# Attention heads in pairs through a three-step loop, with bias, scale and maximum fused, in a float32 transformer kernel

## What is computed

```python
def global_gqa(q, k, v):                 # 8 heads, 2 key heads, all 256 keys
    s = einsum(q, k) * d ** -0.5
    p = softmax(s, axis=-1)
    return einsum(p, v)

def window_gqa_sink(q, k, v, sink):      # 8 heads, only keys within 128 tokens
    s = where(valid, einsum(q, k) * d ** -0.5, -inf)
    m = maximum(s.max(-1, keepdims=True), sink)
    p = exp(s - m)
    p = p / (p.sum(-1, keepdims=True) + exp(sink - m))
    return einsum(p, v)

def mixer_ab(h, ...):                    # layer 0: both kinds of head, side by side
    return concatenate([global_gqa(...), window_gqa_sink(...)]) @ w_out

def mixer_c(h, w_in, w_out, rpb):        # layer 1: 16 heads, neighbourhood of the
    s = einsum(q, k) * d ** -0.5 + bias  # 64-wide grid, bias by relative position
    return einsum(softmax(s), v) @ w_out

def memory_attn(h, mem, ...):            # both layers: 4 heads of width 256
    return einsum(softmax(einsum(q, k) * 256 ** -0.5), v) @ w_o

for i in range(2):                       # the second block
    x = layer_norm(alpha * x + 0.5 * swiglu(x))
    x = layer_norm(alpha * x + (mixer_ab(x) if i == 0 else mixer_c(x)))
    x = layer_norm(alpha * x + memory_attn(x, mem))
    x = layer_norm(alpha * x + 0.5 * swiglu(x))
```

## Time and profile before

| | |
|---|---|
| three executions, median | 2832.29 us (2828.89 to 2833.37) |
| the profiled execution, its own time | 2827.79 us |
| its span in the trace | 2826.3 us |
| TensorE busy | 2672.8 us, 95% |
| VectorE, ScalarE, GpSimd busy | 66%, 51%, 6% |
| granted TensorE clock, mean | 0.979 of full |

### The profile page before, as it was taken

The page is one execution under the profiler, slowest core; times in us unless marked ns, Lnnn a source line. Parts: engine busy times, 40 slices in busy tenths (PEclk is TensorE's granted clock), DMA queues, the critical chain, the costliest instruction groups (busy, mean ns, idle before and its releaser), DMA issues.

```text
span 2826.3 us, 30383 instructions
## 1 busy us (share of the span) xinstructions
PE 2672.8 (95%) x12593; PEld 2169.4 (77%) x12593; DVE 1867.2 (66%) x1877; ACT 1437.8 (51%) x1495; POOL 159.9 (6%) x161
## 2 busy tenths in 40 slices
PE   7999996999999999999998998899999999899998
PEld 5788774878787777778786886597887887678886
DVE  4655565888887887888787557556555544754644
ACT  4444344767676676767674444434443343534432
POOL 2200120000000000000000002000000004200000
PEclk9999997999999999999999999899999999999999
DMA  6555443999998999999996544054655547244652
GB/s 234 182 188 187 159 165 132 364 312 365 318 365 306 349 332 313 359 314 364 309 364 225 198 160 164 16 209 164 200 187 170 203 135 207 92 149 149 208 183 70
DMA packets 451171, 640.75 MB, mean 227 GB/s; under 512 B 16084, under 2 KB 358144, under 8 KB 451024
## 3 DMA queue, kind: packets, MB, share of 16 engines
q1 hardware_dynamic: 444528, 618.52, 64.3%
q0 software_dynamic: 6496, 20.20, 2.5%
HBM read 637.61 MB, written 1.05 MB: 226 GB/s over the span
## 4 chain that ended last, share of the span: by engine, by line
PE 82%; DVE 11%; ACT 4%; DMA 2%; issue 1%; POOL 0%; SPq 0%; DVEq 0%
PE bank L475 25%; PE bank L477 25%; PE bank L476 25%; DVE part_lo L464 5%; ACT part_hi L456 2%; PE bank L964 1%; PE bank L782 1%; DMA raw<-in_c_w_in_dram 1%; PE bank L635 1%; PE bank L1006 1%; PE bank L487 1%; PE bank L808 1%; DMA raw<-in_w_in_dram 1%; DVE x_rows L1967 1%; POOL rstd L2022 0%
## 5 line engine op out<-in xcount | busy, mean ns | idle before, releaser
L464 DVE TENSOR_TENSOR part_lo<-raw,part_hi 128x2048 fp32r<-128x2048 f32 x587 | 1335.7, 2294 | 397.1 <-ACT part_hi L456 396.8
L456 ACT ACTIVATE part_hi<-raw 128x2048 fp32r<-128x2048 f32 x587 | 1107.5, 1911 | 46.4 <-DMA raw<-in_c_w_in_dram 18.4
L475 PE MATMUL bank<-part_hi,x_hi 128*128 128x512 f32 x1088 | 446.1, 410 | 17.8 <-DVE part_lo L464 14.1
L477 PE MATMUL bank<-part_hi,x_lo 128*128 128x512 f32 x1088 | 435.6, 400 | 0.0
L476 PE MATMUL bank<-part_lo,x_hi 128*128 128x512 f32 x1088 | 433.8, 399 | 0.0
L475 PE MATMUL bank<-part_hi,hT_hi 128*128 128x512 f32 x888 | 351.8, 396 | 19.2 <-DVE hT_lo L1438 19.0
L475 PE MATMUL bank<-part_hi,expert_in_hi 128*128 128x512 f32 x896 | 364.4, 407 | 1.6 <-DVE expert_in_lo L1438 1.6
L476 PE MATMUL bank<-part_lo,expert_in_hi 128*128 128x512 f32 x896 | 355.9, 397 | 0.0
L477 PE MATMUL bank<-part_hi,expert_in_lo 128*128 128x512 f32 x896 | 355.5, 397 | 0.0
L476 PE MATMUL bank<-part_lo,hT_hi 128*128 128x512 f32 x888 | 350.4, 395 | 0.0
L477 PE MATMUL bank<-part_hi,hT_lo 128*128 128x512 f32 x888 | 348.2, 392 | 0.0
(11 more groups left out here) (263 smaller groups left out, 2730.2 us busy)
## 6 DMA issues: line engine op xcount, KB each, us to landing
raw<-in_exp_w_gate_dram SPq DMA_DIRECT2D x224, 512.0 KB, 4.9
raw<-in_exp_w_up_dram SPq DMA_DIRECT2D x224, 512.0 KB, 6.6
raw<-in_exp_w_down_dram SPq DMA_DIRECT2D x112, 1024.0 KB, 7.0
raw<-in_ffn_w_gate_dram SPq DMA_DIRECT2D x110, 512.0 KB, 3.8
raw<-in_ffn_w_up_dram SPq DMA_DIRECT2D x110, 512.0 KB, 5.1
raw<-in_ffn_w_down_dram SPq DMA_DIRECT2D x55, 1024.0 KB, 4.9
raw<-in_w_in_dram SPq DMA_DIRECT2D x20, 1024.0 KB, 5.2
raw<-in_mem_w_kv_dram SPq DMA_DIRECT2D x16, 1024.0 KB, 5.1
```

The source lines that it names most:

```text
L456: p.nc.scalar.activation(p.part_hi[i][:, :], p.raw[i][:, :], ACT.Copy).then_inc(*self.rounded.step((name,)))
L464: p.nc.vector.tensor_tensor(p.part_lo[i][:, :], p.raw[i][:, :], p.part_hi[i][:, :].bitcast(F32), ALU.subtract).then_inc(*self.split.step(( ...
L475: nc.tensor.matmul(out, stat_hi, move_hi, start=start, stop=False, skip_group_check=True)
L477: return nc.tensor.matmul(out, stat_lo, move_hi, start=False, stop=stop, skip_group_check=True)
```

## The change

The heads of `ab` and `c` go through the loop in pairs (`PAIRS`), those of `mem` singly (`SINGLES`). An item, a pair or a single head, goes through three steps in place of four, and a fourth buffer `p3` is added. Scores are made one item ahead. In a pair the two heads' score matmuls alternate, and so do the two heads' products with v. On VectorE one `tensor_tensor_reduce` for each 256 columns takes the place of scale and bias, maximum and negation: it makes -scale * (scores + bias) and its running minimum, which is minus the maximum. So the bias and the masks carry a factor 8 (for `c` GpSimd multiplies each head's bias first, one more operation for each of the 16 heads), heads without a bias add a constant zero, the sink comes in as the minimum's start, and `Exp` reads `p` for all heads, where it read the bank for heads without a bias. The other work in the loops is placed anew, by item; in `c` the first three parts of the q projection stand behind the second pair's scores, where they stood behind the first head's. The out projection takes its four weight blocks by the half of `cat` that they multiply, and then by the half of the output columns. It stays behind the loop: `pe_out_early` and the argument `early` are new and no stage uses them.

```diff
 NFF = D_FF // FC
 AHEAD = 4
...
-        self.ring.square_blocks(st, [(w, c, kh) for w, c in blocks + [(wo, 0), (wo, 512)] for kh in range(2)])
+        self.ring.square_blocks(st, [(w, c, kh) for w, c in blocks for kh in range(2)]
+                                + [(wo, c, kh) for kh in range(2) for c in (0, 512)])
...
+def pe_scores(p, st, heads, item):
...
-    hd, b = heads[i], 4 + i % 2
-    for key in hd["ready"]:
-        pe.wait_ge(*p.s.at(*key))
-    if i >= 2 and heads[i - 2]["bias"] is None:
-        pe.wait_ge(*p.s.at("soft", st, i - 2))
-    elif i >= 2:
-        pe.wait_ge(*p.v.at("biased", st, i - 2))
+    for i in item:
+        for key in heads[i]["ready"]:
+            pe.wait_ge(*p.s.at(*key))
+        if i >= 2:
+            pe.wait_ge(*p.v.at("biased", st, i - 2))
     for qt in range(TT):
-        for j, (q, k) in enumerate(hd["terms"]):
-            mm = nc.tensor.matmul(p.bank[b][:, qt * T:(qt + 1) * T], q[:, qt * P:(qt + 1) * P], k,
-                                  start=(j == 0), stop=(j == len(hd["terms"]) - 1), skip_group_check=True)
-    mm.then_inc(*p.t.step(("scores", st, i)))
...
+    for i in item:
+        pe.wait_ge(*p.s.at("pT", st, i))
...
+    for j in range(heads[item[0]]["out"][2]):
         for kt in range(TT):
-            mm = nc.tensor.matmul(p.bank[b][rows, j * T:(j + 1) * T], hd["v"](kt, j), pT[i % 2][:, kt, :],
-                                  start=(kt == 0), stop=(kt == TT - 1), skip_group_check=True)
-    mm.then_inc(*p.t.step(("weighed", st, i)))
...
+            for i in item:
+                b, rows, parts = heads[i]["out"]
+                mm = nc.tensor.matmul(p.bank[b][rows, j * T:(j + 1) * T], heads[i]["v"](kt, j), pT[i % 2][:, kt, :],
+                                      start=(kt == 0), stop=(kt == TT - 1), skip_group_check=True)
...
+def pe_attention(p, st, heads, items, prob, pT, meanwhile):
+
+    m = len(items)
+    pe_scores(p, st, heads, items[0])
+    for j in range(m + 2):
+        if j + 1 < m:
+            pe_scores(p, st, heads, items[j + 1])
+        if j >= 2:
+            pe_weigh(p, st, heads, pT, items[j - 2], items[j - 4][-1] if j >= 4 else None)
+        if 1 <= j <= m:
+            pe_turn_p(p, st, prob, items[j - 1])
+        for part in meanwhile.get(j, ()):
             part()
-        if 2 <= i <= n + 1:
-            pe_turn_p(p, st, i - 2, prob)
-        if i >= 4 and heads[i - 4]["flush"]:
-            flushed[heads[i - 4]["out"][0]] = i - 4
-        if 3 <= i < n + 3:
-            pe_weigh(p, st, i - 3, heads[i - 3], pT, flushed.get(heads[i - 3]["out"][0]))
-    p.pe.wait_ge(*p.v.at("cat_parts", st, n - 1))
...
     q0, q1 = (pe_transposed_half(p, st, 8, b, 2, "qT") for b in range(2))
     k0, k1 = (pe_transposed_half(p, st, 10, b, 3, "kT") for b in range(2))
     meanwhile = {
-        0: [lambda: first(0), *q0[0:2]], 1: q0[2:3], 2: q0[3:4],
-        3: [lambda: first(1), k0[0]], 4: k0[1:2], 5: k0[2:4],
-        6: [lambda: second("qT", 0), *q1[0:2]], 7: q1[2:4],
-        8: [lambda: second("kT", 0), *k1[0:2]], 9: k1[2:3], 10: k1[3:4],
+        0: [lambda: free("kT", 0, 0), *q0[0:3]], 1: [q0[3], lambda: free("kT", 0, 1), *k0[0:2]], 2: k0[2:4],
+        3: [lambda: free("qT", 1, 0), *q1], 4: [lambda: free("kT", 1, 0), *k1],
     }
...
             for qt in range(TT):
-                src = p.bank[b][:, qt * T:(qt + 1) * T] if hd["bias"] is None else P_[:, qt, :]
-                made = nc.scalar.activation(P_[:, qt, :], src, ACT.Exp, bias=p.att_stats[:, i, 0, qt:qt + 1],
-                                            scale=scale if hd["bias"] is None else 1.0,
-                                            accum_out=p.att_stats[:, i, 1, qt:qt + 1])
+                made = nc.scalar.activation(P_[:, qt, :], P_[:, qt, :], ACT.Exp, bias=p.att_stats[:, i, 0, qt:qt + 1],
+                                            scale=-1.0, accum_out=p.att_stats[:, i, 1, qt:qt + 1])
...
+    m = len(items)
+    for j in range(m + 3):
+        for i in items[j] if j < m else ():
+            hd = heads[i]
             dve.wait_ge(*p.t.at("scores", st, i))
-            if hd["bias"] is None:
-                nc.vector.tensor_reduce(top, p.bank[b][:, :].rearrange("p (q k) -> p q k", q=TT), AX.X, ALU.max).then_inc(
-                    *p.v.step(("max", st, i)))
-                dve.wait_ge(*p.v.at("max", st, i))
-                nc.vector.tensor_scalar(top, top, -scale, None, ALU.mult).then_inc(*p.v.step(("top", st, i)))
-            else:
-                if hd["bias_ready"] is not None:
-                    dve.wait_ge(*p.g.at(*hd["bias_ready"]))
-                if i >= 3:
-                    dve.wait_ge(*p.t.at("p_turned", st, i - 3))
-                for qt in range(TT):
-                    bias = hd["bias"](qt)
-                    rows = lambda ap: ap.rearrange("p (m w) -> p m w", w=bias.shape[2])
-                    made = nc.vector.scalar_tensor_tensor(
-                        out=rows(P_[:, qt, :]), in0=rows(p.bank[b][:, qt * T:(qt + 1) * T]), scalar=scale,
-                        in1=bias, op0=ALU.mult, op1=ALU.add)
-                made.then_inc(*p.v.step(("biased", st, i)))
-                dve.wait_ge(*p.v.at("biased", st, i))
-                nc.vector.tensor_reduce(top, P_[:, :, :], AX.X, ALU.max).then_inc(*p.v.step(("max", st, i)))
-                dve.wait_ge(*p.v.at("max", st, i))
-                if hd["sink"] is None:
-                    nc.vector.tensor_scalar(top, top, -1.0, None, ALU.mult).then_inc(*p.v.step(("top", st, i)))
-                else:
-                    nc.vector.tensor_scalar(top, top, hd["sink"], -1.0, ALU.max, ALU.mult).then_inc(*p.v.step(("top", st, i)))
...
+            if hd["bias_ready"] is not None:
+                dve.wait_ge(*p.g.at(*hd["bias_ready"]))
+            if i >= 4:
+                dve.wait_ge(*p.t.at("p_turned", st, i - 4))
             for qt in range(TT):
...
+                bias = hd["bias"](qt)
+                rows = lambda ap: ap.rearrange("p (m w) -> p m w", w=bias.shape[2])
+                made = nc.vector.tensor_tensor_reduce(
+                    out=rows(prob[i % 4][:, qt, :]), in0=rows(p.bank[4 + i % 2][:, qt * T:(qt + 1) * T]), in1=bias,
+                    scale=-scale, scalar=3e38 if hd["sink"] is None else hd["minus_sink"], op0=ALU.add, op1=ALU.min,
+                    accum_out=p.att_stats[:, i, 0, qt:qt + 1])
+            made.then_inc(*p.v.step(("biased", st, i)))
...
     for h in range(C_HEADS):
-        nc.gpsimd.tensor_tensor(bias[:, h, :, :], bias[:, h, :, :],
-                                p.const("neighbours").unsqueeze(1).to_broadcast([P, BIAS_ROWS, GRID_W]), ALU.add).then_inc(
+        view = bias[:, h, :, :]
+        nc.gpsimd.tensor_scalar(view, view, HD ** 0.5, None, ALU.mult).then_inc(*p.g.step(("wide_bias", st, h)))
+        pool.wait_ge(*p.g.at("wide_bias", st, h))
+        nc.gpsimd.tensor_tensor(
+            view, view, p.const("neighbours").unsqueeze(1).to_broadcast([P, BIAS_ROWS, GRID_W]), ALU.add).then_inc(
             *p.g.step(("bias", st, h)))
```

244 lines of the change are left out of this document (124 added, 120 removed).

## The result

The changed kernel took 2783.51 us (median of four, 2781.57 to 2786.30), the kernel before 2832.83 (four, 2828.89 to 2834.76). The ratio is 0.9828, 95% interval 0.9811 to 0.9845: 49 us faster, where 20 were forecast and 2800 to 2828 was the range. Its profiled execution took 2785.18 us, with a span of 2784.0, 42.3 less than the span of before.

The account below looks back on a forecast made before the run. No engine was seen to fill the loops: heads' steps wait for each other and TensorE's clock falls at times. Terms -9 (`ab`), -11 (`c`) and 0 (the rest) took the median 2832.3 to 2812 us, range 2800 to 2828.

Parts of the forecast that it names:

- The rest: 0.: Outside the `ab` and `c` loops: `mem` 0, between -1 and +2 us each; reordered out projection 0; masks' factor nothing.
- The loop of `ab`: Attention loop of `ab`: later start, then shorter pair steps ending at 1814.3 instead of 1825.9, 11.6 us less, forecast -9.
- the 2.6 us kept back for one more stretch at the low clock: Loop of `ab`: allowance taken off the 11.6 us gain for low clock beyond what the steps hold, leaving -9.
- the lower bound of 0.39: VectorE's fused operation: at least 0.39 us each, from the scale-and-bias operation, accumulator row hidden; 0.50 was taken.
- Bound by VectorE.: Pair step of the loop: about 4.2 us, bound by VectorE with ScalarE and TensorE close behind; `ab` took 8.6 a pair.
- The loop of `c`: Attention loop of `c`: TensorE idle 8.7 us at the start, steps 14 us shorter in all, 3 kept back, forecast -11.
- (1): Rival: VectorE's fused operation runs at the scan's rate, 0.76 us each; gain only -7.5, 2825 us; chance 0.10.
- (2): Rival: pairing gains no overlap, TensorE stays at 5.3 to 5.7 us a pair; about -6, 2826 us; chance 0.08.
- (3): Rival: clock stays at 1.2 GHz through the fast steps, each 6.3 us, not 4.2; +5, 2837 us; chance 0.08.
- (5): Rival: GpSimd's 16 additional operations stop VectorE for their whole 26 us, taking `c`'s gain away; 2823 us; chance 0.05.
- neither stopped dead there: Argument against GpSimd stopping VectorE in `c`: long subtraction and adds stand in the same microseconds, yet neither stopped.
- (4): Rival: more gain, fused operation 0.44 us, no additional low clock, weighing at 1.1; -30, 2802 us; chance 0.12.

Follow-up runs that it names:

- before_shift: The kernel before with 64 bytes of unused memory in front of the ring of weight buffers; ratio 0.9961 to the kernel before.
- after_noshift: The changed kernel with its two small new buffers put behind all others, so the weight ring lies where it lay before; ratio 0.9892 to the kernel before.
- the unfused kernel: The changed kernel with the fused operation undone (scale and bias, maximum and negation again), pairs and steps kept; ratio 0.9910 to the kernel before.
- after_no_multiply: The changed kernel without GpSimd's 16 multiplications of the bias in `c`; ratio 0.9843 to the kernel before.
- after_64: The changed kernel with 96 more bytes ahead of the weight ring, its buffers at 64 from a multiple of 128; ratio 0.9786 to the kernel before.
- after_aligned: The changed kernel with 32 more bytes in front of the weight ring, its buffers at multiples of 128 bytes; ratio 0.9746 to the kernel before.

## Why the prediction was wrong, by its steps

**"The rest: 0."** This step took the result out of the range: without the shift the change is at 0.9892, which is 2802 us and inside it. Nothing outside the loops was priced but the order of the out projection and `mem`. `mem` was near (+0.3 each); the out projections lost 1.6 and 1.8 us to the low clock, which the 0 had not allowed for. Two buffers of 64 bytes together (the change's lines `self.minus_sink = put("minus_sink", [P, 8])` and `self.zero = put("zero", [P, 1])`, which I had left out even of the diff shown ahead of the prediction) move the 9 blocks of the weight ring and all behind them, and that alone is worth 11 us (before_shift) to 18 (after_noshift); the traces support the lower end. No row of before shows it; that it was taken for nothing without a bound was the mistake.

**The loop of `ab`: -9 forecast, -19.8 measured.** This is the largest single miss, 10.8 us, and the trace divides it. The starting point was right: rotations of 6.0 us, TensorE idle behind them, low clock. But the first step ended 15.1 us into the loop and not 18.1: four fused operations took 1.4 us, not 2.0, for each of the two pairs that stand ahead of it, and the step itself was shorter. The next three steps, forecast at 6.0, 4.8 and 4.0, took 4.5, 4.7 and 5.6, the same in sum, by luck. The last five took 18.8 us, not 24.0. The forecast had put a whole subtraction or rounding of 2.2 on top of two of them, but none took over 4.8: the first subtraction fell into the step before and cost it 0.9, the second fell into time in which VectorE would have waited. And the 2.6 us kept back for one more stretch at the low clock did not come. Mis-sized as terms were the fused operation (0.50 taken; 0.35 without and 0.41 with a sink measured, the first kind under the lower bound of 0.39) and the pair's products (1.3 taken, 1.08 measured).

**"Bound by VectorE."** A step of 4.2 us was forecast and 4.5 to 4.7 measured, near enough, but for another reason: TensorE and VectorE take turns in a ring of waits over the four buffers of p, and VectorE is idle 0.9 to 2.0 us in each step that has no subtraction. And what fusion does in `ab` was missed altogether. Its price was put at 1.63 - 1.00 a head of VectorE's time; the unfused kernel loses 17 us in `ab`, 7 of them in heads that save next to nothing on VectorE; there the trace shows the scores waiting for `Exp` to free their bank.

**The loop of `c`: -11 forecast, -14.9 measured** (the steps' own sum was 14). Its mechanism held: second scores waiting for VectorE, here 6.2 us and not 8.7, as the loop starts 28 us earlier and lies otherwise against the subtraction; the two multiplications at 0.9 to 1.7 us beside GpSimd (1.98 assumed); bias in time. That the sum of the steps came so near is partly luck: the first step was 2.2 us shorter than forecast, the next four 1.0 shorter, and the last five, in part at the low clock, 2.4 longer.

**The rivals.** (1), the fused operation at the scan's rate: no, 0.35 to 0.41 each. The Trainium skill's rule on two float32 inputs in SBUF ("Vector Engine (DVE) Microarchitecture Reference", "Points that are easy to get wrong"), by whose letter this rival would not occur with one input in PSUM, is not contradicted; no fused operation here had both inputs in SBUF. (2), no overlap: no, 1.14 and 1.08 at full clock, even without alternation. (3), the low clock through the fast steps: it lasted over some steps of each loop (0.89 and 0.84 granted), and did not decide. (5), GpSimd stopping VectorE for all its length: no, after_no_multiply is no faster, and VectorE's multiplications lose 5.9 us and not 26. But "neither stopped dead there" was a misreading. The 25.9 us of 16 merged additions in the earlier trace rows hide two kinds, about 1.0 us alone and over 3 us when one begins during a subtraction:

```profile
L2124 POOL TENSOR_TENSOR bias<-bias,consts x16: 987/1026/3133, 2396.1 to 2421.0; 128x384 f32<-128x384 f32 x16
```

(4), more gain, came nearest: 34 us in the loops, 30.6 with the out projections' loss, against 30. The rest of the distance was the ring's 64 bytes.

## What to carry to other kernels

When a change adds or resizes a buffer, compare the start times of the same instructions in stretches that it doesn't touch, before crediting the change with the whole difference; and try the placement for itself, since here 32 bytes of padding gave 23 us, where two rewritten loops gave 34. Price a fused operation not only by its engine's time but by which buffer or bank it frees, and how much earlier. Where a step is a ring of waits, taking one wait away shows the next at once: look at the loop's length, not at the wait. And before a mean from a merged row enters an estimate, look whether it mixes two kinds: the 1.6 us of an addition above was 1.0 or 3.0.

## What the runs showed of the hardware

- Matmuls of 512 columns with `x` start 234.2, 233.0, 229.6 and 228.1 ns apart with the weight ring at 32, 96, 64 and 0 bytes from a multiple of 128 (before, before_shift, after_64, after_aligned; no difference in work). In the kernel before, 96 is worth 11 us and 0 is worth 39 us against 32. With `hT` 32 bytes off and the ring at 0 the matmuls with `hT` start 233.0 ns apart, in place of 227.2. Which access is slowed, TensorE's reads or others beside them, was not tried.
- Two heads' matmuls on different halves of the rows or columns run at once when they stand behind one another with no wait between, whether they alternate or not: 1.14 and 1.08 us for eight records (1.14 and 1.09 one head after the other), as for four.
- A VectorE operation with a minimum as accumulator over 256 columns, one input from PSUM and one from SBUF, starts every 0.35 us without and 0.41 with a start value from memory, and its accumulator's write is hidden. The row of 0.48 spans more than the interval, so lengths of rows must not be added.
- VectorE's subtraction (two inputs from SBUF) or multiplication and GpSimd's operations on the bias take turns: the one that starts second ends 0.15 us (multiplication) or 1.03 us (GpSimd's multiplication) behind the first. The fused operation, with one input from PSUM, keeps its 0.35 us.
- In the changed kernel the out projection of `ab` begins at the low clock, behind the short idles of the last steps; in the kernel before it began at full clock. Its first matmul, and one four microseconds later:

```profile
1799.42 0.62 PE L481 MATMUL bank<-part_hi,cat_hi 128*128 128x512 f32 x1 [0.93 <-DVE cat_lo L1449]
...
1803.17 0.39 PE L481 MATMUL bank<-part_hi,cat_hi 128*128 128x512 f32 x1
```
